# Down projection of the prompt by seven products of halves, its weight sums made by accumulating DMAs

## The reference

```
h = rmsnorm(x, norm_ffn_g)
gt, ffn_buf_new = causal_dwconv(h @ w_gate, ffn_buf, ffn_conv_w)
x = x + (jax.nn.silu(gt) * (h @ w_up)) @ w_down
```

## Time and profile before

| | us |
|---|---|
| median of three runs | 945.42 |
| span of the profiled execution | 943.7 |
| PE busy | 931.8 |
| DVE busy | 648.3 |
| ACT busy | 452.1 |
| POOL busy | 170.0 |

### The profile page before, as it was taken

How to read it: one execution, slowest core, us unless ns; L and a number is a source line. 1 busy time by engine, 2 the same in 40 slices (tenths; PEclk the granted TensorE clock), 3 DMA queues, 4 the chain that set the end, 5 groups by cost and what they waited for, 6 DMA issues and landing times.

```text
span 943.7 us, 16891 instructions
## 1 busy us (share of the span) xinstructions
PE 931.8 (99%) x6919; PEld 841.9 (89%) x6919; DVE 648.3 (69%) x1083; ACT 452.1 (48%) x836; POOL 170.0 (18%) x198
## 2 busy tenths in 40 slices
PE   9999999999999999999999999999999999999998
PEld 7899888998889877799888999999999999888886
DVE  7627888777775565552666999999999999435321
ACT  6634454648566454554654445444444445333310
POOL 0071101103664331000002032222222220000000
PEclk9999999999999999999999999999999999999999
DMA  8624142121104084244904322222222224412221
GB/s 303 225 88 145 54 168 93 47 94 49 45 5 135 2 290 154 82 142 157 317 18 138 113 87 90 90 90 90 88 73 74 79 89 152 147 64 93 78 89 56
DMA packets 73820, 103.70 MB, mean 110 GB/s; under 512 B 2576, under 2 KB 53904, under 8 KB 73360
## 3 DMA queue, kind: packets, MB, share of 16 engines
q1 hardware_dynamic: 73744, 102.63, 32.6%
HBM read 92.27 MB, written 10.35 MB: 109 GB/s over the span
## 4 chain that ended last, share of the span: by engine, by line
PE 51%; DVE 3%; ACT 2%; POOL 1%; issue 1%; ACTq 0%; POOLq 0%; DVEq 0%
PE bank L1222 8%; PE bank L1220 8%; PE bank L1221 8%; PE bank L538 5%; PE bank L537 5%; PE bank L536 5%; PE bank L484 2%; PE bank L486 1%; PE bank L485 1%; PE bank L466 1%; PE bank L562 1%; PE bank L1034 1%; PE bank L564 1%; PE bank L563 1%; PE bank L1036 1%
## 5 line engine op out<-in xcount | busy, mean ns | idle before, releaser
L2168 DVE TENSOR_TENSOR wlo<-wraw,whi 128x2048 fp32r<-128x2048 f32 (+1 forms) x56 | 126.2, 2253 | 102.2 <-ACT whi L1617 93.0
L1617 ACT ACTIVATE whi<-wraw 128x2048 fp32r<-128x2048 f32 (+1 forms) x58 | 109.3, 1885 | 101.9 <-PE bank L538 72.8
L498 PE MATMUL bank<-hhi,whi 128*128 128x320 f32 x352 | 116.4, 331 | 0.6 <-issue 0.6
L500 PE MATMUL bank<-hhi,wlo 128*128 128x320 f32 x352 | 108.7, 309 | 0.0
L499 PE MATMUL bank<-hlo,whi 128*128 128x320 f32 x352 | 108.7, 309 | 0.0
L498 PEld LDWEIGHTS bank<-hhi,whi 128*128 128x128 f32 x352 | 66.2, 188 | 5.0 <-issue 3.6
L499 PEld LDWEIGHTS bank<-hlo,whi 128*128 128x128 f32 x352 | 66.2, 188 | 3.0 <-issue 2.4
L500 PEld LDWEIGHTS bank<-hhi,wlo 128*128 128x128 f32 x352 | 66.1, 188 | 0.0
L536 PE MATMUL bank<-whi,hhi 128*128 128x512 f32 x150 | 58.4, 389 | 0.0
L537 PE MATMUL bank<-wlo,hhi 128*128 128x512 f32 x150 | 58.4, 389 | 0.0
L538 PE MATMUL bank<-whi,hlo 128*128 128x512 f32 x150 | 58.3, 389 | 0.0
(11 more groups left out here) (491 smaller groups left out, 2690.4 us busy)
## 6 DMA issues: line engine op xcount, KB each, us to landing
wraw<-in_w_in SPq DMA_DIRECT2D x13, 1024.0 KB, 5.5
wraw<-in_w_gate SPq DMA_DIRECT2D x11, 1024.0 KB, 5.2
wraw<-in_w_up SPq DMA_DIRECT2D x11, 1024.0 KB, 5.1
wraw<-in_w_down SPq DMA_DIRECT2D x10, 1024.0 KB, 5.1
kTs<-in_cache_sb_k SPq DMA_DIRECT2D x8, 512.0 KB, 4.4
vraw<-in_cache_sb_v SPq DMA_DIRECT2D x8, 512.0 KB, 4.9
wraw<-in_w_mix_out SPq DMA_DIRECT2D x4, 1024.0 KB, 6.3
kmT<-in_cache_mem_k SPq DMA_DIRECT2D x8, 512.0 KB, 6.2
```

Of the source, the lines that this page charges most:

```text
L498: T.matmul(o, wh[:, k, cs], hhi[:, k, hs], start=(k == 0), stop=False)
L500: ins = T.matmul(o, wl[:, k, cs], hhi[:, k, hs], start=False, stop=(k == KD - 1))
L1617: V(wv(whi, i), wv(wraw, i), ACT.Copy).then_inc(s["w_hi_ready"], 1)
L2168: V.tensor_tensor(wv(wlo, i), wv(wraw, i), wv(whi, i).bitcast(F32), ALU.subtract)\
```

## The change

The down projection of the 512 prompt tokens is done by seven products of halves instead of eight: two halves of 256 tokens, two halves of 11 feature tiles, two halves of 512 columns. The 128 sample tokens are multiplied directly, as before. It goes in two passes of 11 steps. A step of pass 1 does p1, the samples, p3 and p5 in eight banks; a step of pass 2 does p6, p7, p4 and p2. The last two steps are done product by product.

Of the sums of weights that this takes, four 1408 x 512 arrays are made in DRAM by DMAs that POOL issues: 16 plain copies of a quarter of an array (352 rows of 2 KB), one after each of the 16 items of the attention part, and 16 accumulating DMAs, two after each `weight_sums("up", j)`, j from 2 to 9. The sums of `act` are made by POOL (step 0 and 1) and DVE (2 to 10), partly in place. The low parts of `w_down` and of the sums are written over the raw values; raw and high buffers are four deep each.

```
@@ tensor
+            for i in range(HF):
+                pe.wait_ge(s["parts_lo"], i + 1)
+                lo_cut(pe, B_DN[i])
+                product("p1", i, dn_parts(i, 0), dn_weights(i, 0, 0))
+                samples(i)
+                pe.wait_ge(s["sums_lo"], i + 1)
+                product("p3", i, dn_parts(i, 512), dn_weights(i, 1, 1))
+                pe.wait_ge(s["t1_lo"], i + 1)
+                ins = product("p5", i, dn_parts(i, 256), (t1_hi[t1_slot(i)][:, :], t1_lo[t1_slot(i)][:, :]))
...
+            SECOND = (("p6", 0, 1, 0), ("p7", 256, 1, 1), ("p4", 768, 0, 1), ("p2", 512, 0, 0))
+            for i in range(HF - 2):
...
+                for name, p0, a, c in SECOND:
+                    ins = product(name, i, dn_parts(d, p0), dn_weights(d, a, c))
...
+            for name, p0, a, c in SECOND:
+                for t in range(2):
+                    for i in (HF - 2, HF - 1):
...
+                        product(name, i, dn_parts(d, p0), dn_weights(d, a, c), ts=(t,))
@@ sync
             def load_w(i):
+                    if d == 3:
+                        filled(sp, (("up", FT // 2 - 1), "p5"))
+                    else:
+                        passed(sp, i - 3 if d < 3 else i - 4)
...
+            load_t1(0)
+            load_t1(1)
+            for d in range(2, 2 * HF):
+                if d == 4:
+                    passed(sp, B_DN[0])
+                    passed(sp, gu_block("up", FT // 2 - 1))
                     sp.wait_ge(s["rows_kept"], 16)
                     D(xres[:, :, :], kept).then_inc(s["rows_back"], 16)
+                load_w(B_DN[d])
+                if d < HF:
+                    load_t1(d)
@@ gpsimd
+            for x, n in enumerate(past):
                 evacuated(pool, ("z", n, 0))
...
                 ins.then_inc(s["past_ready"], 1)
+                copy_quarter(*copies[x])
...
             for j in SEVEN["gate"]:
                 weight_sums("up", j)
+                if j in (2, 3, 4, 5):
+                    pool.wait_ge(s["weight_rows"], 16 * len(copies))
+                    add_quarter(1, j - 2, quarter_rows(0, 1, j - 2))
+                    add_quarter(3, j - 2, quarter_rows(1, 1, j - 2))
+                elif j in (6, 7):
+                    pool.wait_ge(s["weight_rows"], 16 * 6 * QUARTER_PARTS)
+                    for q in (2 * j - 12, 2 * j - 11):
+                        add_quarter(2, q, sum_rows(3, q))
...
@@ scalar
+                cut_hi(28 + 2 * j)
                 if j == FT // 2 - 1:
-                    for n in range(LEAD):
-                        act_hi(n)
-                cut_hi(28 + 2 * j)
+                    cut_parts(0)
+                    cut_t1(0)
...
+            for d in range(1, 2 * HF):
+                cut_parts(d)
+                cut_hi(B_DN[d])
+                if 1 < d <= HF:
+                    cut_sums(d - 1)
+                if d < HF:
+                    cut_t1(d)
@@ vector
+            sums_lo(0)
+            t1_low(0)
+            for d in range(1, 2 * HF):
+                if BY_POOL <= d < HF:
+                    first_sum(d)
+                parts_lo(d)
+                if BY_POOL <= d < HF:
+                    third_sum(d)
+                if 1 < d <= HF:
+                    sums_lo(d - 1)
+                cut_lo(B_DN[d])
+                if BY_POOL <= d < HF:
+                    second_sum(d)
+                if d < HF:
+                    t1_low(d)
+                if BY_POOL <= d < HF:
+                    fourth_sum(d)
...
+            last_rows()
```

More of the change, by code:

```diff
@@ L1254, in _, with product @@
                         across((kind, j), gu_block(kind, j), hhi, hlo)
-            def ready_a(h, k):
-                pe.wait_ge(s["alo_ready"], FT * h + k + 1)
-            def left_a(h, k):
-                return act_slots(FT * h + k)
-            down("dn", 0, B_DN[0], left_a, NT, ready_a)
-            down("dn", 1, B_DN[1], left_a, NT, ready_a)
+            def product(name, i, stationary, moving, ts=(0, 1), first=0, last=HF - 1):
+                for t in ts:
+                    c = slice(stationary[2] + t * P, stationary[2] + t * P + P)
+                    hi, lo = stationary[0][:, c], stationary[1][:, c]
+                    if i == first:
+                        take((name, t))
+                    o = bank[use[name, t][0]][:, :]
+                    T.matmul(o, hi, moving[0], start=(i == first), stop=False)
+                    T.matmul(o, hi, moving[1], start=False, stop=False)
+                    ins = T.matmul(o, lo, moving[0], start=False, stop=(i == last))
+                    if i == last:
+                        done(ins, (name, t))
+                return ins
@@ new lines, in dn_parts, with dn_weights, samples @@
+            def dn_parts(m, c):
+                hi, lo = part_hi[part_slot(m)], part_lo[part_slot(m)]
+                return hi, lo, c
+            def dn_weights(d, a, c):
+                cs = slice(512 * c, 512 * c + 512)
+                return wv(whi, B_DN[d])[:, a, cs], wv(wlo, B_DN[d])[:, a, cs]
+            def samples(i):
+                hi, lo = part_hi[part_slot(i)], part_lo[part_slot(i)]
+                for c in range(2):
+                    if i == 0:
+                        take(("cs", c))
+                    o = bank[use["cs", c][0]][:, :]
+                    for a in range(2):
+                        ss = slice(768 + a * P, 768 + a * P + P)
+                        wh, wl = dn_weights(i, a, c)
+                        T.matmul(o, hi[:, ss], wh, start=(i == 0 and a == 0), stop=False)
+                        T.matmul(o, hi[:, ss], wl, start=False, stop=False)
+                        ins = T.matmul(o, lo[:, ss], wh, start=False, stop=(i == HF - 1 and a == 1))
+                    if i == HF - 1:
+                        done(ins, ("cs", c))
@@ new lines, in _ @@
+            for i in range(HF):
[7 more added lines that the diff above has]
+                ins = product("p5", i, dn_parts(i, 256), (t1_hi[t1_slot(i)][:, :], t1_lo[t1_slot(i)][:, :]))
+                if i < HF - 1:
+                    step(ins, B_DN[i])
+                else:
+                    ends[B_DN[i]] = ("bank", ("p5", 1))
@@ L2839, in _, with to_rows, free, first_rows @@
-            for n in range(NT):
-                add_res("dn", 1, n)
+            def to_rows(name, t, n, c, op=ALU.add):
+                b, x = filled(dve, (name, t)), xres[:, n, 512 * c:512 * c + 512]
+                return V.tensor_tensor(x, x, bank[b][:, :], op)
+            def free(ins, name, t):
+                ins.then_inc(bank_free[use[name, t][0]], 1)
+            def first_rows():
+                dve.wait_ge(s["rows_back"], 16)
+                for c in range(2):
+                    free(to_rows("cs", c, PT, c), "cs", c)
+                for t in range(2):
+                    free(to_rows("p3", t, t, 1), "p3", t)
```

312 lines of the change are left out of this document (245 added, 67 removed).

## The result

| | before | changed |
|---|---|---|
| median of the runs, us | 945.19 (4 runs, 944.78 to 945.74) | 928.64 (4 runs, 928.51 to 929.18) |
| span of the profiled execution | 943.7 | 926.8 |

The ratio is 0.9826, with a 95% interval of 0.9814 to 0.9838: 16.55 us less.

The account below looks back on a forecast made before the run. PE was taken as the bound, busy 931.8 of 943.7 us. Span 943.7 - 14.96 (matmuls) + 0.3 (start of the stage) = 929.0; the median of runs lies 1.7 above, so 930.8; range 929.3 to 941.

Parts of the forecast that it names:

- Matmuls removed: Down projection: 594 matmuls instead of 660 at an unchanged 0.2267 us each, clock 1.00, so 14.96 us less.
- The low end: Bottom of the range, 929.3 us: only the matmuls can be gained, 945.42 - 14.96 = 930.5 less the spread of runs.
- Cost taken: 0: The sum's term for DMAs that POOL issues in attention and gate and up: they cost PE nothing.
- Start of the stage: Down projection's first steps: DVE's cut of block 1 could make PE wait 0 to 1.1 us; 0.3 taken.
- Pass 1: Down projection's first pass: DVE needs 6.2 us a step against PE's 6.80, gaining 0.6 a step if never waiting.
- Step 4: Pass 1, block loaded behind the residual rows: cost 0 with 0.7 us to spare; 2 to 3 if transfers take a quarter longer.
- Pass 2 and the end: Down projection's second pass: DVE's at most 4.6 us hidden in 5.44 a step; one addition behind PE as before: cost 0.
- DMAs on POOL: Attention, gate and up: issues of 1 to 3 us, a copy 4.3, an accumulation up to 9.1; cost 0.
- 1: Gate and up: slow accumulations hold POOL, deciding from 10.7 us each; at 12 us, 21 us lost, 952; chance 0.10.
- 2: Gate and up's weight loads or block 4 behind residual rows come 2 to 6 us late: 933 to 940; chance 0.13.
- 3: Pass 1: DVE becomes the bound at 7.3 us a step, 5.5 over 11 steps: 936; chance 0.09.
- 4: Attention part: POOL's issues cost most, some 16 x 1 us, little or nothing gained: 941 to 947; chance 0.04.

Follow-up runs that it names:

- g2: The kernel before, with POOL filling eight values of a spare tile and waiting for itself after the first attention item, no DMA: 944.33 us (one run).
- f1: The changed kernel with no edit, run again beside later variants: 929.16 us, ratio to before 0.9828.
- f4: The changed kernel, with DVE filling a free 128x1024 buffer twice just ahead of its cut of block 1 of w_down: 931.21 us.
- f3: The changed kernel with four accumulating DMAs a period of gate and up instead of two, each period also waiting for those before: 984.53 us, ratio to before 1.041.
- g4: The changed kernel with 2048 instead of 1024 bytes a partition for descriptors of POOL's DMAs: 929.54 us, ratio to before 0.9830.
- e2: The kernel before with the change's 16 copies and 16 accumulating DMAs on POOL, their sums unused, down projection unchanged: 944.35 us, ratio 0.9988.
- g3: The changed kernel, with matmuls of the high parts first per weight block in the memory projections (w_mk, w_mv): 928.78 us, ratio to before 0.9826.
- h1: The changed kernel with g3's order and the last token rows' transposes moved behind the first quarter of the second w_mk block's low parts: 927.23 us, ratio 0.9808.
- e1: The kernel before, with POOL filling 512 values of traw_up just ahead of the weight sums of up 2: 944.79 us, ratio 0.9990.

## Why the prediction was right and wrong

- **Matmuls removed**: 14.96 forecast, 593 steps of 0.2267 us measured, 14.96 less. Right, clock 1.00 included.
- **The low end, "nothing but the matmuls can be gained"**: this step failed. The gain outside the matmuls was put at nothing and measured 1.30 us, the turns of POOL and DVE. The sum on the spans is 943.7 - 14.96 (matmuls) - 1.30 (POOL's and DVE's turns) - 0.52 (before 288 us, by chance) - 0.11 (tail: 3.69 to 3.58 behind PE's last start) = 926.8. The range ended at 929.3, so it took both the 1.30 and the chance of the 0.52 to come out 0.7 below it; the same kernel came out at 929.16 and 929.32 later, on either side of that end. That it missed by 0.7 and not by nothing is luck, that it gained 1.3 us unforeseen is not. I counted PE's waits as too small to matter and took the longest, 1.4. The right question was which of them hangs on a race that an edit elsewhere can turn. Three more rows of before said so: the 1.1 us wait for tlo_gate; nine of these low parts, of which the median is 1.758 us and one took 2.671; and POOL and DVE 0.02 us apart at 541. The way there was in my sum, as "Cost taken: 0" for POOL's DMAs. Cost 0 was right, gain 0 was not (though g2 shows that a single fill would have gained it too).
- **Start of the stage, +0.3**: measured 0, with 0.90 us (first profile) and 0.50 us (f1) to spare. ACT cut the weight sum ahead of the silus at 785.37, as forecast; f4 shows that this place binds as soon as the cover is used up.
- **Pass 1**: DVE 5.9 us a step, no wait of PE. Step 4 was the narrow place, as forecast, and had more room: DVE's low part of the sums of step 3 stands at 810.32 with 0.69 us, wanted by PE 18 matmuls into step 3, at 809.18 + 4.08 = 813.3. 2.3 us instead of 0.7, since the block landed earlier.

```profile
807.86 1.92 ACT L1823 ACTIVATE dn_hi<-dn_raw 128x2048 fp32r<-128x2048 f32 x1 [4.23 <-DMA dn_raw<-in_w_down]
809.68 0.61 ACT L2306 ACTIVATE part_hi<-part_raw 128x512 fp32r<-128x512 f32 x1
```

- **Pass 2 and the end**: right. One addition is behind PE's last matmul, as in the earlier trace rows, and DVE was idle ahead of it:

```profile
922.29 0.69 DVE L3123 TENSOR_TENSOR xres<-xres,bank 128x512 f32<-128x512 f32 x1 [0.60 <-PE bank L1326]
923.65 0.69 DVE L3123 TENSOR_TENSOR xres<-xres,bank 128x512 f32<-128x512 f32 x1 [0.67 <-PE bank L1326]
```

- **DMAs on POOL**: an issue takes 0.60 to 0.81 us for a copy and 0.92 to 0.99 for an accumulation. By the medians a quarter lands in 5.2 us as a copy (twelve of them; the first four took 8.0, and I had 4.3), and in 7.2 to 9.2 as an accumulation (up to 9.1). The weight loads beside them kept their 5.1 to 5.3 us. The accumulations among the DMA issues from 200 us on (KB each, median us to landing):

```profile
weight_sums<-weight_sums POOLq DMA_DIRECT2D x8, 704.0 KB, 7.6
first_weight_sum<-in_w_down POOLq DMA_DIRECT2D x4, 704.0 KB, 7.2
weight_sums<-in_w_down POOLq DMA_DIRECT2D x4, 704.0 KB, 9.2
```

The rule of the Trainium skill ("DMA: Bandwidth & Descriptors", section on SWDGE, HWDGE and iDMA) that VectorE can lock out the writing of descriptors showed in no accumulation: each was issued in 0.92 to 0.99 us while DVE was busy for 22.34 of 24.64. But every DVE instruction beside them was a TENSOR_TENSOR, so for its other operations no run here says anything. The same page's figures gave an estimate of 3.7 us a quarter; the trace has 5.2 and 8.0. What would have helped is a sentence of the Trainium skill's "GPSIMD Engine Reference" (section Key points): POOL's way into SBUF is shared with DVE, with contention where a DVE instruction has two SBUF inputs. The low parts are such instructions, and the trace agrees: 0.9 to 1.5 us for the one behind, at up 2.
- **Rivals**: 1 did not come, but f3 shows that it was nearer than I held. My decision point of 10.7 us an accumulation counted only idle time; the wait for room (g4) takes another 6 us of POOL, and two more a period cost 57 us. 2 and 3 did not come, with the margins above. 4: the selects were up to 2.2 us later, and PE lost nothing (e2 against before).

## What to carry to other kernels

Where an instruction group has one member well above its median, and the other engine's operation begins within a few tenths of a microsecond of it, treat it as a race that any edit can turn, and put its price at both ends of the range, on the gain side too. When a few tenths matter, compare distances between two marks of unchanged work in the profiles rather than run times: here they were good to 0.1 us, once the granted clock between the marks was known to be the same (it was not in g3). And in a kernel that PE bounds, matmuls that need only the high part can be put first, so that a late low part is hidden; then look at what PE now reaches too early (g3 against h1).

## What the runs showed of the hardware

- POOL's and DVE's TENSOR_TENSOR on two SBUF operands take turns. The second waits for most of the first: DVE's low part takes 2.67 us instead of 1.76, POOL's operation 2.75 or 2.80 instead of 1.30. A fill of POOL, which reads nothing, made DVE wait for nothing: 1.76 beside it in e1.
- POOL's second accumulating DMA of 704 KB stands 5.7 to 6.9 us with no semaphore to wait for, with 1024 bytes a partition for descriptors; with 2048 it stands 0 (g4). The same edit takes away the 4.82 us that POOL stands ahead of the third plain copy of the changed kernel. So the wait is for room, and it blocks all of POOL.
- In f3 PE paused for 39 us in 8 periods, 4.9 in each by the mean, and the granted clock was at a mean of 0.89 to 0.95 in six of seven stretches of 30 to 34 us from 600 to 822 us (1.00 in the seventh, and in the stretch ahead of them, without a pause), so part of each was spent at 1.2 instead of 2.4 GHz. The loss of 57 us is that of POOL's list, which bounds these periods; the slower clock added nothing to it.
- The time from the start to 288 us differs by up to 1.5 us from one execution to another, part of it in gaps on PE with nothing to wait for: none near 268 us in the first profile of the changed kernel, 0.86 in the next two of the same kernel.
- In one of 18 profiles (g3) the granted clock was 0.86 by the mean from 288 to 300 us, so part of this stretch was spent at 1.2 instead of 2.4 GHz, and 1.56 us were lost, in a part where its program is that of the changed kernel.
